# A two-layer diffusion block on one core: the first norm's squares, the first modulation step and the order of H's remainders are rearranged

## The reference, cut to what matters

```python
def rmsnorm(x, g):
    xf = x.astype(jnp.float32)
    y = xf * lax.rsqrt(jnp.mean(xf * xf, axis=-1, keepdims=True) + EPS)
    return (y * g.astype(jnp.float32)).astype(x.dtype)

def adaln(cvec, w, b):
    m = jax.nn.silu(cvec) @ w + b
    m = m.reshape(-1, 1, 6 * D_MODEL)
    return jnp.split(m, 6, axis=-1)
...
        sh1x, sc1x, g1x, sh2x, sc2x, g2x = adaln(c, ada_w[i], ada_b[i])
        sh1c, sc1c, g1c, sh2c, sc2c, g2c = adaln(c_ctx, ada_w[i], ada_b[i])
        hx = rmsnorm(x, norm1_g[i]) * (1 + sc1x) + sh1x
        hc = rmsnorm(ctx, norm1_g[i]) * (1 + sc1c) + sh1c
        (qn_x, qr_x, kn_x, kr_x, v_x), rest_x = mixer_features(hx, *feat_w, rope)
        (qn_c, qr_c, kn_c, kr_c, v_c), rest_c = mixer_features(hc, *feat_w, None)
...
    q_lat, kv_lat, k_rope, pool_in, gate_b, gate_c, conv_in = jnp.split(h @ w_in, IN_SPLITS, axis=-1)
```

## Time and profile before

| quantity | value |
|---|---|
| median of 3 runs | 1554.69 us (1546.18 to 1557.04) |
| the profiled execution's own time | 1551.67 us |
| its span | 1549.9 us |
| mean granted TensorE clock | 0.989 |
| TensorE busy | 1458.5 us, 94% |
| VectorE busy | 1030.1 us, 66% |
| ScalarE busy | 539.0 us, 35% |
| latents of layer 0, first to last matmul | 27.99 to 85.75 us |

### The profile page before, as it was taken

The page is one execution under the profiler, slowest core; times in us unless marked ns, Lnnn a source line. Parts: engine busy times, 40 slices in busy tenths (PEclk is TensorE's granted clock), DMA queues, the critical chain, the costliest instruction groups (busy, mean ns, idle before and its releaser), DMA issues.

```text
span 1549.9 us, 21266 instructions
## 1 busy us (share of the span) xinstructions
PE 1458.5 (94%) x8112; PEld 1247.3 (80%) x8112; DVE 1030.1 (66%) x1559; ACT 539.0 (35%) x819; POOL 70.7 (5%) x107
## 2 busy tenths in 40 slices
PE   3898889999999999999999998988899999999998
PEld 2687777787978888888888878876789888888887
DVE  5458787668985666566656578767757655556555
ACT  4252466424322212121212224455534333332331
POOL 0023110000000000000000000320000000000000
PEclk9999999999999999999999999999999999999999
DMA  9533100131553433343224321410011323322234
GB/s 387 207 106 135 37 9 9 68 123 55 173 183 119 129 115 96 106 135 122 95 95 149 108 68 37 136 37 8 0 55 55 109 90 103 106 95 95 81 108 135
DMA packets 43264, 157.99 MB, mean 102 GB/s; under 512 B 5200, under 2 KB 6608, under 8 KB 42064
## 3 DMA queue, kind: packets, MB, share of 16 engines
q1 hardware_dynamic: 43216, 157.35, 30.3%
HBM read 155.23 MB, written 2.10 MB: 102 GB/s over the span
## 4 chain that ended last, share of the span: by engine, by line
PE 76%; DVE 15%; issue 4%; ACT 3%; DMA 2%; POOL 0%; DVEq 0%; SPq 0%; ACTq 0%; POOLq 0%
PE ps L595 56%; PE ps L544 6%; PE ps L545 5%; PE ps L546 5%; DVE ada_out L1187 2%; DVE w_lo L1172 2%; DVE tmp L1263 1%; DVE H_lo L1272 1%; DVE qkt L1447 1%; DVE ss L1254 1%; DVE ss L1234 1%; DMA w_raw<-in_w_main 1%; DVE prob L1494 1%; PE ps L558 1%; DVE pt_lo L1278 1%
## 5 line engine op out<-in xcount | busy, mean ns | idle before, releaser
L595 PE MATMUL ps<-H_hi,w_hi 128*128 128x512 f32 (+1 forms) x1280 | 391.9, 355 | 12.4 <-DVE tmp L1373 5.0
L595 PE MATMUL ps<-H_lo,w_hi 128*128 128x512 f32 (+1 forms) x1280 | 387.5, 351 | 0.0
L595 PE MATMUL ps<-H_hi,w_lo 128*128 128x512 f32 (+1 forms) x1280 | 387.1, 351 | 0.0
L888 ACT ACTIVATE w_hi<-w_raw 128x1024 fp32r<-128x1024 f32 x174 | 181.5, 1057 | 444.8 <-PE ps L595 388.5
L1285 DVE SCALAR_TENSOR_TENSOR X<-ps,mod,X 128x512 f32<-128x512 f32 (+1 forms) x296 | 181.7, 646 | 117.9 <-PE ps L595 87.3
L595 PEld LDWEIGHTS ps<-H_hi,w_hi 128*128 128x128 f32 x1280 | 215.0, 189 | 47.5 <-issue 8.7
L595 PEld LDWEIGHTS ps<-H_lo,w_hi 128*128 128x128 f32 x1280 | 216.2, 190 | 35.1
L595 PEld LDWEIGHTS ps<-H_hi,w_lo 128*128 128x128 f32 x1280 | 213.9, 189 | 34.2
L1172 DVE TENSOR_TENSOR w_lo<-w_raw,w_hi 128x1024 fp32r<-128x1024 f32 x174 | 215.8, 1251 | 32.4 <-ACT w_hi L888 29.4
L1609 DVE SCALAR_TENSOR_TENSOR tmp<-ps,vec,tmp 128x511 f32<-128x511 f32 (+1 forms) x132 | 87.2, 661 | 133.4 <-ACT tmp L1144 125.7
L595 PE MATMUL ps<-inner_hi,w_hi 128*128 128x512 f32 (+1 forms) x528 | 164.0, 360 | 3.3 <-DVE X L1285 1.4
(11 more groups left out here) (177 smaller groups left out, 1989.0 us busy)
## 6 DMA issues: line engine op xcount, KB each, us to landing
w_raw<-in_w_main SPq DMA_DIRECT2D x176, 512.0 KB, 3.3
ada_raw<-in_w_ada SPq DMA_DIRECT2D x73, 512.0 KB, 4.2
ada_step<-in_w_step SPq DMA_DIRECT2D x7, 2048.0 KB, 13.8
hw_raw<-in_w_head SPq DMA_DIRECT2D x8, 320.0 KB, 2.9
X<-in_x SPq DMA_DIRECT2D x2, 1024.0 KB, 6.8
cb<-in_cvec SPq DMA_DIRECT2D x2, 1024.0 KB, 8.3
out_x<-X SPq DMA_DIRECT2D x8, 256.0 KB, 4.7
rtab<-in_rope SPq DMA_DIRECT2D x4, 384.0 KB, 6.0
```

What stands on the lines that cost most here:

```text
L595: ins = pe.matmul(job.ps(a, b), ww[:, wsl], xx[:, xk, a:b], start=first and n == 0, stop=last and n == 2)
L888: act.activation(w_hi[c % 4][:], w_raw[c % 2][:], ACT.Copy).then_inc(chunk_hi, 1)
```

## The change

- Three of the eight squared tiles (1, 3 and 5) go to buffers of their own (`squares`), and TensorE adds them into the norm's sum by six more matmuls with `ones`, ahead of those over `ss`. VectorE adds only the other five.
- On the load queue, modulation step 0 stands ahead of the first weight chunk.
- On TensorE, the rows of step 1 stand ahead of piece 0 of the latents, where they stood ahead of piece 1.
- On ScalarE, `split_hi(0)` stands behind the two roots of the norm. On VectorE, `split_lo(0)` stands behind the first reciprocal.
- On VectorE, `low` of the pieces 2, 4 and 6 stands ahead of `scaled` (with its `modulation`) of the piece after it; it stood behind.

```diff
+    squares = [at(f"squares{n}", lo_free + 4 * KD * NT + 4 * NT * n, [P, NT]) for n in range(3)]
...
-    ROWS_AT, COPY_AT, TURN_AT = (1, 3, 5, 8, 11, 14), (1, 3, 5, 9, 12, 15), (2, 4, 6, 10, 13, 16)
+    ROWS_AT, COPY_AT, TURN_AT = (0, 3, 5, 8, 11, 14), (1, 3, 5, 9, 12, 15), (2, 4, 6, 10, 13, 16)
+    PE_SQUARES = (1, 3, 5)
+    DVE_SQUARES = (0, 2, 4, 6, 7)
...
+        load_step(0)
         load(0)
-        load_step(0)
         load_step(1)
...
-            pe.wait_ge(ss_done[nn], 2 + (KD if nn == 0 else (KD + 4 * (nn % 2), 2 * KD)[n]))
-            return pe.matmul(out, ones[:], ss[:, a:b], start=True, stop=True)
+            pe.wait_ge(ss_done[nn], 2 + (len(DVE_SQUARES) if nn == 0 else (KD + 4 * (nn % 2), 2 * KD)[n]))
+            return pe.matmul(out, ones[:], ss[:, a:b], start=nn > 0, stop=True)
...
+        for e in range(len(PE_SQUARES)):
+            pe.wait_ge(square_done, e + 1)
+            for n, (_, a, b) in enumerate(nsegs(0)):
+                pe.matmul(Job(JOB["sum", 0][n]).ps(a, b), ones[:], squares[e][:, a:b], start=e == 0, stop=False)
...
-            square(0, m, m, 0, NT)
-        split_hi(0)
+            if m in PE_SQUARES:
+                act.activation(squares[PE_SQUARES.index(m)][:], X[:, m], ACT.Square).then_inc(square_done, 1)
+            else:
+                square(0, DVE_SQUARES.index(m), m, 0, NT)
         for n in range(2):
             root_job(0, n)
+        split_hi(0)
         rows_out(0)
...
+            if nn == 0 and n == 0:
+                split_lo(0)
             if nn == 0 and kk % 2 == 0 and kk not in [p[0] for p in work[:n]]:
                 modulation(kk // 2)
...
-        for m in range(KD):
-            add_squares(0, m, 0, NT)
-        split_lo(0)
+        for e in range(len(DVE_SQUARES)):
+            add_squares(0, e, 0, NT)
...
                 for n in range(len(pieces(0))):
+                    turns = n + 1 in (3, 5, 7)
+                    if turns:
+                        low(0, n)
                     if n + 1 < len(pieces(0)):
                         scaled(0, n + 1)
-                    low(0, n)
+                    if not turns:
+                        low(0, n)
```

More of the change, by code:

```diff
@@ L228, in build @@
     cb_in, cb_ok = sem("cb_in"), sem("cb_ok")
+    square_done = sem("square_done")
     vec_in, x_in, tab_in, csil_done = sem("vec_in"), sems("x_in", 2), sem("tab_in"), sem("csil_done")
```

## The result

| | before | changed |
|---|---|---|
| median, 8 runs each | 1554.28 us (1546.18 to 1557.04) | 1537.66 us (1530.52 to 1544.44) |
| ratio of the runs, 95% interval | | 0.9913 (0.9886 to 0.9941) |
| profiled execution: span | 1549.9 us | 1534.6 us |
| mean granted clock | 0.989 | 0.986 |

The ratio means 13.5 us of 1554.28, 0.87% (by its interval, 9.2 to 17.7 us); the medians themselves are 16.6 apart. The forecast gain was 13.2, the forecast time 1541.5, which is 3.8 above the measured median. The two profiled executions are 15.3 us apart: 12.9 up to the a2 stage, as shown next, and 2.4 behind it.

The account below looks back on a forecast made before the run. TensorE carries 76% of the chain, so time can come only from where it stands or runs slowly. 12.2 + 2.5 - 1.4 - 0.2 = 13.1, said as 13.2 us, gives a forecast median of 1541.5 us, range 1534 to 1550.

Parts of the forecast that it names:

- Part 1: First latents matmul to rows of step 4: 12.2 us from moved rows, three gaps and three half-clock stretches, before deductions.
- Part 2, the front: Squares and norm sum up to the rows of step 0: these start at 17.95 instead of 20.45, 2.5 us gained.
- squares that bind: Rival: TensorE's squares bind the front, which gives 0 to 0.5 us; gain 10.8, time 1543.9; chance 0.14.
- The low clock in spite of the recorded 1.00: Norm sum at 17.50 to 20.40: TensorE ran at 1.2 of 2.4 GHz; 1.00 taken at its word gives 0.3 us.
- One slow stretch: Before the first latents piece: one of three half-clock stretches stays, 2.8 us long, costing 1.4 us.
- Loads: Modulation steps land when they did; only step 1 is late, its rows 23.0 to 25.0, covered with 0.4 us to spare.
- Part 3: Behind the latents, from 64.80 on: everything hangs on progress, so the gain reaches the end undiminished.
- The marks named: Signs of being right: rows of step 0 near 18.0, no gap before pieces 2, 4, 6, a2 stage unchanged in length.
- The sum: Whole kernel: 12.2 + 2.5 - 1.4 - 0.2 = 13.1 us gained, said as 13.2 with rounding.
- loads that bind beyond step 1: Rival: loads bind the earlier stage, its steps wanted 3 to 15 us sooner; 3 to 4 us lost, 1545; chance 0.10.
- a clock that sinks in the dense stretch: Rival: clock at 0.50 from first piece to end of latents, 16 us slower, 1571; chance 0.02.
- more than forecast: Rival: no slow stretch, a shorter turn, later clock falls vanishing; gain 15.5 to 17 us, 1538 with spread; chance 0.22.

Follow-up runs that it names:

- e1: Kernel before with only VectorE's new order, remainders of pieces 2, 4 and 6 ahead of the next piece's modulation; ratio to the kernel before 0.9932.
- e2: Changed kernel with VectorE's old order, remainders of pieces 2, 4 and 6 behind the modulation again; ratio to the kernel before 0.9944.
- e6: Changed kernel plus five idle TensorE matmuls in the waits around the turn of step 0; ratio to the kernel before 0.9934, median 1543.79 us.
- e7: As e6, with the rows of step 4 ahead of piece 7 instead of piece 8; ratio to the kernel before 0.987, median 1537.07 us.
- e10: e7 once more, unchanged, beside e9 on one chip; median 1533.05 us, ratio to the kernel before 0.988.
- e9: Changed kernel once more, unchanged, for a second profile and comparison; median 1538.97 us, ratio to the kernel before 0.993.
- e5: Changed kernel with the first weight chunk ahead of modulation step 0 again on the load queue; one execution, 1544.24 us.
- e8: Kernel before, unchanged, for a second profile; one execution, 1552.26 us.
- e3: Changed kernel with all eight squares added by VectorE, as before; ratio to the kernel before 0.9922.

## Why the prediction was right, step by step

- **Part 1** (12.2, less 0.2 for piece 7): measured 36.8 to 24.7, that is 12.1. The gaps went through VectorE's order, as e1 and e2 show from both sides. That it fits to 0.1 is in part luck: the wait before piece 7 was 0.39, not 0.2, and the three turns held TensorE for 0.8 each (the next matmul starts at 30.52 behind the turn at 29.72), not for the 0.95 of the sum. The cover of piece 7 was rightly named as the short one.
- **Part 2, the front** (2.5 on the rows of step 0): 1.5 in the profile at hand, 2.0 in the second, 2.3 to 2.6 in the six other profiles with TensorE's squares. About 0.6 of what is missing is the landing of X (0.7 us late: 8.84 for 8.14 of the first square), which no row of before could tell: VectorE's last add ends at 17.14, not 16.54. The other 0.3 is a step that the prediction had wrong. It let the clock rise in the second square, after about 3 us. Each of the six matmuls over `squares` shows as two records in the profile. Here nine of the twelve records come before full rate, three behind it (ns min/median/max):

```profile
L611 PE MATMUL ps<-squares,ones x9: 634/1001/1192, 10.6 to 15.8; 128*128 128x512 f32 x5, 128*128 128x256 f32 x4
```

```profile
L611 PE MATMUL ps<-squares,ones x3: 379/379/593, 16.7 to 17.3; 128*128 128x256 f32 x2, 128*128 128x512 f32 x1
```

Full rate came 6.1 us after the first of them, inside the third square (3.3 to 5.8 us in the seven other profiles), so the sum over `ss` starts at 17.51 with no wait for VectorE in front of it: TensorE's own squares held it, for 0.3 us. This is the rival of the squares that bind, on a small scale. In six of the seven others TensorE waits 0.28 to 1.02 us for VectorE there instead.

- **The low clock in spite of the recorded 1.00** held: three squares took 7.11 us from 10.56, the sum behind them 1.45 against 2.90 in the earlier trace rows. As the Trainium skill has it ("TensorE: Matmul & The Clock Gate", Part 1), activity releases the throttle.
- **One slow stretch** (1.4): it came, on the rows of step 1, 3.39 for 1.92, 1.5 us. It fell where the prediction looked for it. That the idle waits cause it is likely by e6, e7 and e10 (no fall in three profiles, against three in four).
- **Loads:** step 1 was the one late, as foretold, at 23.7 instead of 23.0; the others were in time. The margin of 0.4 us did not hold in the profile at hand. This and the late X are one shift of the queue, not two: in the changed kernel, e9, e2 and e5 the rows of step 1 start 15.0 to 15.1 us behind the first square. Front and slow stretch together were to give 1.1 and gave 0.8.
- **Part 3, all of it reaches the end:** the mark, the distance from rows 4 to the end, was 1485.1 and is 1482.7; in e8 it was 1484.6, in e3 1493.6. It moves by 11 us with things that are no part of the change, the pace of the loop and the granted clock, so it could confirm nothing to a few us. That the marks gain 12.9 and the runs 13.5 and 10.9 is what stands behind it. That the first ratio comes within 0.3 us of the forecast is luck, with an interval of 9.2 to 17.7.
- **The marks named** were early: first latents 25.4 (27.18; 25.97), rows 4 at 50 to 51.5 (51.90; 51.70), the last latents matmul at 71 to 72.5 (starts at 72.63; 72.43).
- **The sum** is 13.1 by its own terms; the 13.2 is not a rounding of it. Nothing hangs on the 0.1.
- **The rivals:** squares that bind (e3: no, but for the 0.3 us above), loads that bind beyond step 1 (no wait elsewhere), a clock that sinks in the dense stretch (1.00 from 28 us to the end of the latents). The argument against this last one had a reading too short: the slow stretch from 37.9 to 40.8 ended after 4.0 us of continuous work (TensorE runs from 36.78 on), not within 3.1. The rival "more than forecast" named the absence of a slow stretch; e6 brought it about on purpose, worth 1.6 to 1.8 us at the first a2 matmul. The 0.8 us of e7 were not among its ways.

## What to carry to other kernels

When an engine waits for the answer to its own question, look at what the answering engine has queued in front of work that is ready: here a remainder that stood behind a modulation cost 2 us three times, and moving it ahead was worth more than half of the change (7.3 of 12.9 us alone). A wait moved to the front of the chain also exposes what lay behind it: count the bytes ahead of each load before expecting the front's gain to pass. Where parts are worth 1 or 2 us and executions differ by 10, compare marks in the profile, not medians, and ask of every difference in the rest whether two profiles of one kernel show it too. Look there at the granted clock and at the pace of a long loop first.

## What the runs showed that was not expected

- TensorE's loop of layer 0 (512 and 256 columns in turn, weights loaded for each) runs at one of two steady paces, 568 or 579 matmuls in 100 us, at full clock and with no idle time. It differs between executions of one kernel (before: 568 and 579), and 3000 matmuls take 8.7 us more at the slow one. What sets it is open.
- The view gives the granted clock as 1.00 before and during the engine's first work, while that work runs at the lower level: the first sum of the kernel before took 2.90 us, the same sum behind the squares 1.45.
- Five idle matmuls in two waits of 0.8 and 1.4 us went with full clock in three profiles of three; without them it fell in three of four.
